# The gate and up products of a mixture of experts with weights stationary and 96 token slots moving, instead of 128 token slots stationary and weights moving

## The chip, the cores and the metric

The kernel runs on one core of a Trainium2 chip. The metric is the device time of one execution in microseconds (us). Lower is better.

## The reference, cut to what matters

The program is one inference step of a two-layer decoder on 280 tokens (16 meta tokens, 256 of a prompt, 8 samples). Each layer has a mixer and a feed-forward part. That of the second layer is a mixture of 8 experts, of which every token uses two:

```python
def swiglu(h, w1, w3, w2):
    return (jax.nn.silu(h @ w1) * (h @ w3)) @ w2

def moe_ffn(h, w_router, w1, w3, w2):
    logits = (h @ w_router).astype(jnp.float32)
    top_v, top_i = lax.top_k(logits, TOP_K)          # TOP_K = 2
    gates = jax.nn.softmax(top_v, axis=-1)
    combine = jnp.sum(jax.nn.one_hot(top_i, N_EXPERTS, dtype=jnp.float32) * gates[..., None], axis=-2)
    ...
    for e in range(N_EXPERTS):                        # 8 experts
        out = out + combine[..., e:e + 1] * swiglu(h, w1[e], w3[e], w2[e])
```

The model is 1024 wide (D), an expert 3584 (DE). All data are 32-bit floats. Counted on the reference's inputs, the eight experts get 67, 55, 68, 77, 73, 61, 77 and 82 tokens.

## The kernel before

**Precision.** For the experts a 32-bit value is split in a high part and a low part, `x = hi + lo`, both of the type fp32r, and a product is made of three matmuls: hi by hi, hi by lo, lo by hi (`split_products`). All matmuls go through the helper `mm` (line 526), so the profile gives them that line; transposes have lines of their own (1055 the gather, 1066 the selection, 1105 the activations). A matmul instruction has a stationary operand, which a weight load (PEld in the profile) brings in, and a moving one, whose columns stream through. Every matmul here has a weight load of its own.

**Stream of weights.** SyncE (SP) loads all weights through a ring of 7 slots of 128x2048 floats (1 MB). An expert has 3 x 14 slots, so the experts have 336. For each slot n ScalarE (ACT) writes the high part `w_hi[n % 4]` (`high`), VectorE (DVE) the low part `w_lo[n % 4]` (`low`) and gives the ring slot back (`weights_used`), and TensorE (PE) uses both. ACT may write `w_hi` for slot n + 4 when PE has finished slot n (`slot_done`).

**Iterations.** The 3584 columns of an expert are cut in 14 groups of FW = 256, so there are 8 x 14 = 112 iterations t. PE's program in one is written out by hand in `one_pass`: `up(t, 0)` and `up(t, 1)` with `turn(t - 1)` between them, then `down(t - 2)`.

- `up`: the gathered tokens of the expert (128 slots, CAP, most of the last ones empty) are stationary as `he_hi` and `he_lo`; the 256 gate and 256 up columns of the weights, side by side, are the 512 moving columns. Each of the two slots holds 4 of the 8 blocks of the contraction: 4 x 3 matmuls. The result is tokens by columns, in one PSUM bank.
- ACT makes silu of the gate half (`silu_out`), DVE multiplies by the up half (`act_out`), and PE turns the product with two transposes (`turn`), since the next product contracts over the columns. ACT and DVE split the turned result in `at_hi` and `at_lo` (`turned_out`).
- `down`: `at_hi` and `at_lo` stationary, 512 weight columns moving: 2 x 2 x 3 matmuls.

Once per expert, in fixed iterations of the 14: result times the token's weight (`y_out`), back to token order and added to x (`combine`, four iterations with 4 more matmuls each), which tokens the next expert gets (`rows_of`, with `select` on GpSimd), the fetch of their rows with an indirect DMA from GpSimd (POOL), and their transposes (`gather`). GpSimd does nothing else in this phase.

If an expert has more tokens than CAP, a second pass over all experts follows (`npass`).

Of the kernel before, what the change touches and what calls it, by code (L numbers as in the profile page):

```python
# [51 lines left out]
CAP = 128  # L52
# [71 lines left out]
def build(nc, a, debug=None):  # L124

    with ExitStack() as ctx:
# [52 lines left out]
        def ar(at, *shape):  # L179
# [4 lines left out]
            if len(shape) == 1:  # L184
# [62 lines left out]
        sil_e, act_e = ar(5504, 2, FW), ar(6016, 2, FW)  # L247
        y_hi, y_lo = half("y_hi", 4480, D), half("y_lo", 11840, D)
        he_hi = [half(f"he_hi{i}", 6720 + 2048 * i, DC, CAP) for i in range(2)]
        he_lo = [half(f"he_lo{i}", 7744 + 2048 * i, DC, CAP) for i in range(2)]  # L250
        at_hi, at_lo = half("at_hi", 10816, 2, 2 * CAP), half("at_lo", 11328, 2, 2 * CAP)

# [14 lines left out]
                 "selp_ready", "h_stored", "rows_ready", "he_in", "ey_hi", "ga_ps", "ga_hi", "ga_lo", "mw_ps", "mw_out", "eup_silu",  # L267
                 "eup_act", "et_ps", "et_hi", "et_lo", "ey_out", "em_ps", "em_out", "weights_used",
# [85 lines left out]
        def _(pool):  # L354
# [115 lines left out]
            def select(e):  # L470
                for m, (t0, nt, _) in enumerate(TILES):
                    ins = nc.gpsimd.tensor_scalar(sel_p[0:nt, m, :], iota[0:nt], place[0:nt, m, e + 1:e + 2],
                                                  chosen[0:nt, m, e + 1:e + 2], ALU.is_equal, ALU.mult)
                return ins
# [6 lines left out]

            def one_pass(p):
                for e in range(E):
                    n = p * E + e
                    if e or not isinstance(p, int):
                        pool.wait_ge(S["mw_ps"], n)
                        tick(p)
                    select(e).then_inc(S["selp_ready"], 1)
                    pool.wait_ge(S["mw_out"], n + 1)
                    tick(p)  # L490
                    if e or not isinstance(p, int):
                        pool.wait_ge(S["ga_ps"], p * (2 * E) + 2 * e)
                        tick(p)
                    else:
                        pool.wait_ge(S["h_stored"], 32)
                    nc.gpsimd.tensor_copy(rows[:], slot_iw[:, e % 2, 0:1]).then_inc(S["rows_ready"], 1)  # L496
                    pool.wait_ge(S["rows_ready"], n + 1)
                    tick(p)
                    nc.gpsimd.indirect_dma_start(he_f, None, h_rows, bass.IndirectOffsetOnAxis(ap=rows[:, 0:1], axis=0),
                                                 bounds_check=T - 1).then_inc(S["he_in"], 16)  # L500
# [23 lines left out]
        def _(pe):  # L524
# [523 lines left out]
            def gather(p, e, half_):  # L1048

                if half_ == 0:  # L1050
                    pe.wait_ge(S["he_in"], p * (16 * E) + 16 * (e + 1))
                    pe.wait_ge(S["em_out"], p * (E * DC) + DC * max(e - 1, 0))
                for j in range(4):
                    c = 4 * half_ + j
                    last = nc.tensor.transpose(pools[acc(e) + half_][:, j * P:(j + 1) * P], he_f[:, c * P:(c + 1) * P], ident[:])
                last.then_inc(S["ga_ps"], 1)

            def rows_of(p, e):

                pe.wait_ge(S["selp_ready"], p * E + (e + 1))  # L1060
                if e or not isinstance(p, int):
                    pe.wait_ge(S["mw_out"], p * E + e)
                for m, (t0, nt, _) in enumerate(TILES):
                    mm(pools[3][:, T:T + 2], sel_p[0:nt, m, :], id_w[0:nt, m, e, :], m == 0, m == 2)
                for m, (t0, nt, _) in enumerate(TILES):
                    last = nc.tensor.transpose(pools[3][:, t0:t0 + nt], sel_p[0:nt, m, :], ident[0:nt, 0:nt])
                last.then_inc(S["mw_ps"], 1)

            def combine(p, e, c0):
# [3 lines left out]
                for c in range(c0, c0 + 2):  # L1073
# [3 lines left out]
                    mm(o, y_hi[:, q], mix_s[e % 2], True, False)  # L1077
                    mm(o, y_lo[:, q], mix_s[e % 2], False, True).then_inc(S["em_ps"], 1)
# [6 lines left out]
            def up(p, t, part):  # L1085
# [4 lines left out]
                if part == 0 and t >= 2:  # L1090
                    pe.wait_ge(S["eup_act"], p * N_ITER + (t - 1))
# [1177 lines left out]
```

## Time and profile before

| | |
|---|---|
| median of 3 runs | 2256.25 us (2254.21 to 2258.53) |
| the profiled execution's own time | 2257.98 us |
| its span, first to last instruction | 2255.8 us |
| mean granted TensorE clock | 0.933 of full speed |
| busy: PE, PEld, DVE, ACT, POOL | 91%, 75%, 70%, 45%, 16% |
| moved from HBM | 459.74 MB |

The span is the time that the profile covers; the run's own time lies 2.2 us above it. A share of busy time is a mean over a mixer, a dense layer, a mixer and the experts, in which different engines matter; the experts take about the last 1020 us. A PE matmul's duration in the profile contains its latency, and the next one starts before it ends, so that the distance from start to start tells what a matmul costs in a stream.

### The profile page before, as it was taken

The page shows a single profiled execution, that of the slowest core. Times are in us where ns is not written, and L with a number is a line of the kernel's source. Part 1 is how long each engine was busy: PE and PEld are TensorE (multiplying, and loading weights), DVE is VectorE, ACT ScalarE, POOL GpSimd, SP SyncE. Part 2 cuts the span into 40 slices and gives each one's busy share as a digit, 9 for nine tenths or more (in the row PEclk, how much of TensorE's full clock was granted, in tenths as well). Part 3 has the DMA queues.
Part 4 walks back from the last instruction along what each step waited for, and adds up shares of the span by engine and source line. Part 5 has one row for each costly group of instructions (what it writes and reads, how often), then busy time and mean ns, then how long its engine had stood idle before and what let it go on. Part 6 is the DMA issues. An engine that isn't in the chain of part 4 may idle for free.

```text
span 2255.8 us, 29759 instructions
## 1 busy us (share of the span) xinstructions
PE 2056.7 (91%) x11490; PEld 1690.4 (75%) x11490; DVE 1573.3 (70%) x1960; ACT 1012.1 (45%) x1184; POOL 359.5 (16%) x315
## 2 busy tenths in 40 slices
PE   3998789898999997788895999999999999999996
PEld 2775577778999775577774888888888888888884
DVE  3586766325544777766324889898988889898984
ACT  1012323104433111333103777777767677777773
POOL 0553600200000554501201010101010100100000
PEclk7997999598999998999695999999999999999998
DMA  6333000144443333000142999999999999999990
GB/s 241 112 114 112 3 1 1 59 166 180 169 168 131 112 131 113 3 1 1 40 167 81 365 377 355 354 362 359 357 364 357 360 366 353 366 360 352 364 361 36
DMA packets 71627, 466.71 MB, mean 207 GB/s; under 512 B 12453, under 2 KB 13349, under 8 KB 16325
## 3 DMA queue, kind: packets, MB, share of 16 engines
q1 hardware_dynamic: 62352, 449.11, 53.7%
q0 software_dynamic: 3184, 13.24, 1.5%
q10 hardware_dynamic: 5956, 2.50, 0.4%
q8 instruction: 93, 1.52, 0.3%
q14 instruction: 42, 0.34, 0.0%
HBM read 459.74 MB, written 5.08 MB: 206 GB/s over the span
## 4 chain that ended last, share of the span: by engine, by line
PE 79%; DVE 7%; issue 6%; POOL 4%; ACT 2%; ACTq 1%; DMA 0%; SPq 0%; DVEq 0%; POOLq 0%
PE bank L526 77%; PE bank L1105 1%; ACTq L1183 1%; POOL arena L376 1%; DVE arena L1660 1%; PE bank L673 1%; ACT arena L1168 1%; POOL arena L390 1%; DVE arena L1490 0%; POOL arena L397 0%; DVE ring L1791 0%; DVE ring L1815 0%; DVE ring L1803 0%; ACT ring L1168 0%; POOL arena L408 0%
## 5 line engine op out<-in xcount | busy, mean ns | idle before, releaser
L2065 DVE TENSOR_TENSOR w_lo<-ring,w_hi 128x2048 fp32r<-128x2048 f32 x336 | 768.9, 2293 | 109.1 <-ACT w_hi L1168 108.7
L1168 ACT ACTIVATE w_hi<-ring 128x2048 fp32r<-128x2048 f32 x336 | 643.5, 1916 | 183.2 <-PE bank L526 183.2
L526 PE MATMUL bank<-arena,ring 128*128 128x280 f32 (+1 forms) x1920 | 460.6, 408 | 48.1 <-DVE arena L1490 23.0
L526 PEld LDWEIGHTS bank<-arena,ring 128*128 128x128 f32 (+1 forms) x1920 | 354.8, 190 | 143.4 <-issue 39.1
L1168 ACT ACTIVATE arena<-bank 128x256 f32<-128x256 f32 (+4 forms) x300 | 117.7, 396 | 592.2 <-PE bank L526 576.5
L526 PE MATMUL bank<-w_hi,he_hi 128*128 128x512 f32 x896 | 365.4, 408 | 4.9 <-DVE w_lo L2065 4.9
L526 PE MATMUL bank<-w_hi,he_lo 128*128 128x512 f32 x896 | 353.8, 395 | 0.0
L526 PE MATMUL bank<-w_lo,he_hi 128*128 128x512 f32 x896 | 353.4, 394 | 0.0
L526 PEld LDWEIGHTS bank<-w_hi,he_lo 128*128 128x128 f32 x896 | 169.0, 189 | 39.3
L526 PEld LDWEIGHTS bank<-w_hi,he_hi 128*128 128x128 f32 x896 | 169.1, 189 | 37.2 <-issue 5.3
L526 PEld LDWEIGHTS bank<-w_lo,he_hi 128*128 128x128 f32 x896 | 169.8, 190 | 32.4
L526 PE MATMUL bank<-ring 128*128 128x128 f32 (+6 forms) x1504 | 163.0, 269 | 31.9 <-DVE ring L1791 14.8
L526 PEld LDWEIGHTS bank<-ring 128*128 128x128 f32 (+3 forms) x1504 | 147.6, 171 | 49.7 <-DVE ring L1791 18.4
L526 PE MATMUL bank<-w_hi,at_hi 128*128 128x512 f32 x448 | 176.4, 394 | 0.0
L526 PE MATMUL bank<-w_hi,at_lo 128*128 128x512 f32 x448 | 176.4, 394 | 0.0
L526 PE MATMUL bank<-w_lo,at_hi 128*128 128x512 f32 x448 | 176.2, 393 | 0.0
L526 PE MATMUL bank<-arena 64*64 64x64 f32 (+12 forms) x1472 | 140.2, 307 | 34.8 <-DVE arena L1601 25.4
L526 PEld LDWEIGHTS bank<-arena 64*64 64x64 f32 (+6 forms) x1472 | 102.9, 179 | 76.5 <-issue 32.5
L1168 ACT ACTIVATE ring<-bank 128x256 f32<-128x256 f32 (+4 forms) x210 | 63.0, 358 | 169.2 <-PE bank L526 133.5
L496 POOL CAST rows<-arena 128x1 uint32<-128x1 f32 x8 | 13.9, 1732 | 763.9 <-ACT arena L1168 763.9
L1981 DVE TENSOR_TENSOR fw_lo<-ring,fw_hi 128x2048 fp32r<-128x2048 f32 x33 | 75.6, 2293 | 61.1 <-ACT fw_hi L1168 61.1
L526 PE MATMUL bank<-h_hi,fw_hi 128*128 128x280 f32 x352 | 103.6, 294 | 11.4 <-DVE fw_lo L1981 11.4
(261 smaller groups left out, 2634.9 us busy)
## 6 DMA issues: line engine op xcount, KB each, us to landing
ring<-wstream_dram SPq DMA_DIRECT2D x427, 1024.0 KB, 6.8
s<-s_dram POOLq DMA_DIRECT2D x2, 1024.0 KB, 14.7
o_rw_dram<-arena POOLq DMA_DIRECT2D x2, 1024.0 KB, 5.1
x<-x_dram SPq DMA_DIRECT2D x1, 1120.0 KB, 5.0
y_dram<-arena POOLq DMA_DIRECT2D x1, 1120.0 KB, 4.4
arena<-s_b_dram POOLq DMA_DIRECT2D x2, 512.0 KB, 7.5
arena<-s_c_dram POOLq DMA_DIRECT2D x2, 512.0 KB, 9.4
arena<-lora_up_dram POOLq DMA_DIRECT2D x2, 512.0 KB, 11.4
```

The lines of the kernel that those rows point to most:

```text
L376: g.tensor_tensor(tc, ca, cb, ALU.mult)
L390: ins = g.tensor_scalar(chi[:, f, :], z[:, 4 + f, :], col(l, "k_k", f), None, ALU.mult)
L496: nc.gpsimd.tensor_copy(rows[:], slot_iw[:, e % 2, 0:1]).then_inc(S["rows_ready"], 1)
L526: return nc.tensor.matmul(out, lhsT, rhs, start=start, stop=stop, **k)
L673: last = nc.tensor.transpose(pools[4 * i][0:nt, j * P:(j + 1) * P], src, ident[:])
L1105: last = nc.tensor.transpose(pools[2][:, (t % 2) * FW + j * P:(t % 2) * FW + (j + 1) * P], act_e[:, t % 2, j * P:(j + 1) * P], ident[:])
L1168: return nc.scalar.activation(out, in_, func, **k)
L1183: ac.dma_start(t[:], a[n]).then_inc(S["consts"], 16)
L1660: ins = v.tensor_scalar(z[:, c, :], z[:, c, :], col(l, "mu", c), None, ALU.mult)
L1981: v.tensor_tensor(fw_lo[n % 2], slot(FFN_AT + n), fw_hi[n % 2].bitcast(F32), ALU.subtract)\
L2065: v.tensor_tensor(w_lo[n % SPLIT], slot(n), w_hi[n % SPLIT].bitcast(F32), ALU.subtract)\
```

## The change

It leaves the rest of the program alone and does this in the expert phase:

- CAP goes from 128 to 96 slots. `he_hi` and `he_lo` become one tile `he` with the 96 high and the 96 low columns side by side for each of the 8 contraction blocks.
- `up` is turned around: a 128x128 block of gate or up weights is stationary. The high part of the block meets `he` whole (192 columns: hi and lo tokens), the low part meets the 96 high columns. `up(t, 0)` takes a slot with gate weights, `up(t, 1)` one with up weights, each 2 blocks of columns by 8 of the contraction. The result is columns by tokens in two banks, the products with the tokens' high part in one half and those with the low part in the other.
- `turn` and its transposes go. Instead the halves have to be added: ACT copies the low half of both banks to `sum_e` (`low_products`), DVE adds the other half (`sum_out`), ACT makes silu (`silu_out`), POOL multiplies (`act_out`), ACT writes `at_hi` (`act_high`), POOL `at_lo` (`act_low`).
- `down` has 96 stationary columns, otherwise as before; so have the other steps of an expert. `rows_of` uses the expert's own banks, and GpSimd's steps (`choose`, `fetch`) have fixed iterations.

```diff
-CAP = 128
+CAP = 96
...
+        he = [half(f"he{i}", 6720 + 1536 * i, DC, 2, CAP) for i in range(2)]
+        at_hi, at_lo = half("at_hi", 10816, 2, 2, CAP), half("at_lo", 11328, 2, 2, CAP)
+        def up_bank(t, u):
+            return pools[2 * (t % 2) + u][:, 0:4 * CAP].rearrange("p (b s t) -> p b s t", b=2, s=2)
+        def up_parts(t, s):
+            both = banks[:, 2 * (t % 2):2 * (t % 2) + 2, 0:4 * CAP]
+            return both.rearrange("p u (b s t) -> p u b s t", b=2, s=2)[:, :, :, s, :]
...
+            def act_out(p, t):
+                pool.wait_ge(S["eup_part"], up_part(p, t, "silu"))
+                nc.gpsimd.tensor_tensor(act_e[:, t % 2], sil_e[:, t % 2], sum_e[:, t % 2, 1], ALU.mult).then_inc(S["eup_act"], 1)
+            def act_low(p, t):
+                pool.wait_ge(S["et_hi"], p * N_ITER + (t + 1))
+                nc.gpsimd.tensor_tensor(at_lo[:, t % 2], act_e[:, t % 2], at_hi[:, t % 2].bitcast(F32), ALU.subtract)\
+                    .then_inc(S["et_lo"], 1)
...
                 if part == 0 and t >= 2:
-                    pe.wait_ge(S["eup_act"], p * N_ITER + (t - 1))
-                w_h, w_l = (w.rearrange("p (k m) -> p k m", k=DC // 2) for w in w_split(p, SLOT_OF[f"up{part}", t]))
-                for c in range(DC // 2):
-                    k = part * (DC // 2) + c
-                    last = split_products(pools[t % 2], (he_hi[e % 2][:, k, :], he_lo[e % 2][:, k, :]),
-                                          (w_h[:, c, :], w_l[:, c, :]), k == 0, k == DC - 1)
+                    pe.wait_ge(S["eup_sum"], p * N_ITER + (t - 1))
+                w_h, w_l = (w.rearrange("p (k m) -> p k m", k=DC) for w in w_split(p, SLOT_OF[f"up{part}", t]))
+                for b in range(2):
+                    o, q = up_bank(t, part)[:, b], slice(b * P, (b + 1) * P)
+                    for k in range(DC):
+                        if k < DC - 1:
+                            mm(o, w_h[:, k, q], he[e % 2][:, k], k == 0, False)
+                        last = mm(o[:, 1], w_l[:, k, q], he[e % 2][:, k, 0], False, False)
+                    last = mm(o, w_h[:, k, q], he[e % 2][:, k], False, True)
                 last.then_inc(S["slot_done"], 1)
-            def turn(p, t):
...
+            def low_products(p, t):
+                ac.wait_ge(S["slot_done"], p * N_SLOTS + (SLOT_OF["up1", t] + 1))
+                fn(sum_e[:, t % 2], up_parts(t, 1), ACT.Identity).then_inc(S["eup_part"], 1)
             def silu_out(p, t):
...
+                ac.wait_ge(S["eup_sum"], p * N_ITER + (t + 1))
+                fn(sil_e[:, t % 2], sum_e[:, t % 2, 0], ACT.Silu).then_inc(S["eup_part"], 1)
+            def act_high(p, t):
+                ac.wait_ge(S["eup_act"], p * N_ITER + (t + 1))
...
+            def sum_out(p, t):
+                dve.wait_ge(S["eup_part"], up_part(p, t, "low"))
+                v.tensor_tensor(sum_e[:, t % 2], sum_e[:, t % 2], up_parts(t, 0), ALU.add).then_inc(S["eup_sum"], 1)
```

**The order on PE.** In the expert phase of the kernel before, from `turn` into the second `up` of an iteration, PE's program reads as follows (the number behind a name is that of the buffer; the three matmuls come four times):

```order
L1105 MATMUL bank<-ident,arena 128x128 [waits et_lo,eup_act]
L1105 MATMUL bank<-ident,arena 128x128
L526 MATMUL bank<-w_hi_59,he_hi_69 128x512 [waits weights_used]
L526 MATMUL bank<-w_lo_63,he_hi_69 128x512
L526 MATMUL bank<-w_hi_59,he_lo_71 128x512
```

In the changed kernel the end of the second `up` of an iteration, `down`, and the start of the next `up` read:

```order
L563 MATMUL bank<-he_69,w_lo_66 128x96 x2
L563 MATMUL bank<-he_69,w_hi_62 128x192
L563 MATMUL bank<-w_hi_59,at_hi 96x512 [waits et_lo,weights_used]
L563 MATMUL bank<-w_lo_63,at_hi 96x512
L563 MATMUL bank<-w_hi_59,at_lo 96x512
L563 MATMUL bank<-he_69,w_hi_60 128x192 [waits weights_used,eup_sum]
L563 MATMUL bank<-he_69,w_lo_64 128x96
```

An `up` call had 12 matmuls of 512 moving columns and has 32, of 192 and 96 columns in turn; the transposes are gone, and `down` still has 12 of 512.

**The order on ACT.** In one iteration ACT had two small steps, one behind the other, among three splits of weights:

```order
L1168 ACTIVATE arena<-bank 128x256 [waits eup_act,slot_done]
L1168 ACTIVATE w_hi_62<-ring 128x2048 [waits slot_done,slot_in1]
L1168 ACTIVATE w_hi_59<-ring 128x2048 [waits slot_done,slot_in2]
L1168 ACTIVATE w_hi_60<-ring 128x2048 [waits slot_done,slot_in3]
L1168 ACTIVATE at_hi<-bank 128x256 [waits slot_done,et_ps]
```

In the changed kernel it has three, each between two splits:

```order
L1199 ACTIVATE arena<-bank 128x384 [waits slot_done]
L1199 ACTIVATE w_hi_62<-ring 128x2048 [waits slot_done,slot_in1]
L1199 ACTIVATE arena<-arena 128x192 [waits eup_sum]
L1199 ACTIVATE w_hi_59<-ring 128x2048 [waits slot_done,slot_in2]
L1199 ACTIVATE at_hi<-arena 128x192 [waits slot_done,eup_act]
L1199 ACTIVATE w_hi_60<-ring 128x2048 [waits slot_done,slot_in3]
```

The third small step now waits for POOL (`eup_act`), whose two new instructions per iteration are, in POOL's program:

```order
L520 TENSOR_TENSOR arena<-arena 128x192 [waits eup_part]
L524 TENSOR_TENSOR at_lo<-arena,at_hi 128x192 [waits et_hi]
L484 TENSOR_SCALAR arena<-iota,arena 128x96 [waits mw_ps]
L484 TENSOR_SCALAR arena<-iota,arena 128x96
L484 TENSOR_SCALAR arena<-iota,arena 24x96
```

The selection of the next expert's tokens (line 484) now stands behind the two small steps of an iteration; before it stood alone.

## Rows read from the trace of the kernel before

**Rows 1.** Busy time by stretch: columns us, PE, PEld, DVE, ACT, POOL, clock, DMA share, GB/s.

```profile
1300.00:2200.00 900.00, 900.00 (x4090) 732.98 (x4090) 801.93 (x593) 656.62 (x549) 57.64 (x32) 1.00 0.96 360
```

**Rows 2.** The chain that ended last, two iterations and a start; start, us, what.

```profile
1362.16 0.22 PE bank L1105 x2
1362.38 8.33 PE bank L526 x36
...
1370.93 8.34 PE bank L526 x36
...
1379.49 8.83 PE bank L526 x40
...
1503.67 8.84 PE bank L526 x40
```

**Rows 3.** Waits from 1300 to 2200 us: who, for whom, us, times, longest.

```profile
ACT w_hi L1168 <- PE bank L526: 168.5, 196, 1.9
DVE w_lo L2065 <- ACT w_hi L1168: 97.8, 277, 1.9
SPq L340 <- DVE w_lo L2065: 715.2, 304, 3.6
```

**Rows 4.** Timeline of PE and of its weight loads behind a turn.

```profile
1503.29 0.38 PE L1105 MATMUL bank<-ident,arena 128*128 128x128 f32 x2
1503.42 0.48 PE L526 MATMUL bank<-w_hi,he_hi 128*128 128x512 f32 x1
...
1503.40 0.19 PEld L526 LDWEIGHTS bank<-w_hi,he_hi 128*128 128x128 f32 x1
1503.51 0.19 PEld L526 LDWEIGHTS bank<-w_lo,he_hi 128*128 128x128 f32 x1
1503.74 0.19 PEld L526 LDWEIGHTS bank<-w_hi,he_lo 128*128 128x128 f32 x1
```

**Rows 5.** Busy time by stretch: the router's small matmuls, the dense layer, two mixer stretches.

```profile
1189.70:1197.30 7.60, 7.58 (x48) 7.56 (x48) 0.27 (x1) 0.00 (x0) 0.00 (x0) 0.50 0.00 0
530.00:700.00 170.00, 170.00 (x1322) 170.00 (x1321) 81.45 (x75) 66.55 (x70) 0.00 (x0) 1.00 0.49 174
290.00:330.00 40.00, 35.35 (x312) 28.68 (x312) 26.05 (x73) 12.53 (x40) 0.00 (x0) 1.00 0.00 1
1104.00:1118.00 14.00, 13.06 (x142) 12.81 (x142) 1.97 (x3) 0.59 (x1) 6.38 (x6) 0.50 0.01 1
```

**Rows 6.** Groups of PE and PEld instructions, whole run: busy, mean ns, idle.

```profile
L526 PE MATMUL bank<-router,arena 128*128 128x8 f32 x32 | 7.0, 362 | 6.1 <-DVE arena L1490 6.1
L526 PE MATMUL bank<-router,arena 128*24 128x8 f32 x16 | 0.8, 189 | 0.0
L526 PEld LDWEIGHTS bank<-w_hi,he_hi 128*128 128x128 f32 x896 | 169.1, 189 | 37.2 <-issue 5.3
L1105 PEld LDWEIGHTS bank<-ident,arena 128*128 128x128 f32 x224 | 31.4, 140 | 15.4
```

**Rows 7.** Timeline of the weight loads of plain 32-bit 128x128 matmuls in a mixer.

```profile
367.89 5.54 PEld L526 LDWEIGHTS bank<-ring 128*128 128x128 f32 x48 [1.26 <-DVE ring L1791]
```

**Rows 8.** Groups of DVE, ACT and POOL instructions, 1300 to 2200 us.

```profile
L2065 DVE TENSOR_TENSOR w_lo<-ring,w_hi 128x2048 fp32r<-128x2048 f32 x305 | 698.2, 2293 | 98.2 <-ACT w_hi L1168 97.8
L1168 ACT ACTIVATE w_hi<-ring 128x2048 fp32r<-128x2048 f32 x305 | 584.5, 1916 | 168.5 <-PE bank L526 168.5
L1168 ACT ACTIVATE arena<-bank 128x256 f32<-128x256 f32 x102 | 39.4, 386 | 75.4 <-PE bank L526 75.4
L1168 ACT ACTIVATE he_hi<-bank 128x512 fp32r<-128x512 f32 x14 | 8.1, 576 | 0.0
L2034 DVE TENSOR_TENSOR he_lo<-bank,he_hi 128x512 fp32r<-128x512 f32 x14 | 9.6, 683 | 0.0
L472 POOL TENSOR_SCALAR arena<-iota,arena 24x128 f32<-24x128 f32 x6 | 14.8, 2459 | 0.0
```

**Rows 9.** Timeline: DVE's splits of weights back to back.

```profile
1501.31 6.69 DVE L2065 TENSOR_TENSOR w_lo<-ring,w_hi 128x2048 fp32r<-128x2048 f32 x3
```

More of the change, by code:

```diff
@@ L480, in tick, with choose @@
                     nc.gpsimd.tensor_tensor(pool_tick[:, k:k + 1], iota[:, 0:1], iota[:, 1:2], ALU.add)
-            def one_pass(p):
[L483 to L500, printed above, removed]
+            def choose(p, e):
+                n = p * E + e
+                if e or not isinstance(p, int):
+                    pool.wait_ge(S["mw_ps"], n)
+                    tick(p)
+                select(e).then_inc(S["selp_ready"], 1)
@@ new lines, in fetch @@
+            def fetch(p, e):
+                n = p * E + e
+                pool.wait_ge(S["mw_out"], n + 1)
+                tick(p)
+                if e or not isinstance(p, int):
+                    pool.wait_ge(S["ga_ps"], p * (2 * E) + 2 * e)
+                    tick(p)
+                else:
+                    pool.wait_ge(S["h_stored"], 32)
+                nc.gpsimd.tensor_copy(rows[0:CAP], slot_iw[0:CAP, e % 2, 0:1]).then_inc(S["rows_ready"], 1)
+                pool.wait_ge(S["rows_ready"], n + 1)
+                tick(p)
+                nc.gpsimd.indirect_dma_start(he_f[0:CAP], None, h_rows, bass.IndirectOffsetOnAxis(ap=rows[0:CAP, 0:1], axis=0),
+                                             bounds_check=T - 1).then_inc(S["he_in"], 16)
@@ new lines, in act_out @@
+            def act_out(p, t):
[5 more added lines that the diff above has]
+                    .then_inc(S["et_lo"], 1)
+            def one_pass(p):
+                choose(p, 0)
+                fetch(p, 0)
+                for t in range(1, N_ITER + 1):
+                    e, g = divmod(t, NG)
+                    act_out(p, t - 1)
+                    act_low(p, t - 1)
+                    if e < E - 1 and g == G_YOUT:
+                        choose(p, e + 1)
+                    if e < E - 1 and g == G_ROWS + 1:
+                        fetch(p, e + 1)
@@ L1060, in rows_of @@
                 pe.wait_ge(S["selp_ready"], p * E + (e + 1))
+                if e >= 2:
+                    pe.wait_ge(S["em_out"], p * (E * DC) + DC * (e - 1))
+                if e == 0 and isinstance(p, int):
+                    pe.wait_ge(S["ht_out"], 6)
                 if e or not isinstance(p, int):
@@ L1432, in one_pass @@
                     if 1 <= t <= N_ITER:
[L1433 removed]
+                        silu_out(p, t - 1)
                     if t < N_ITER:
[L1435 removed]
                         high_after(p, SLOT_OF["up1", t])
+                    if 1 <= t <= N_ITER:
+                        act_high(p, t - 1)
                     if t >= LAG:
@@ L2196, in _stream @@
     assert slots.shape[0] == S_DENSE
-    up = np.stack([i[w][0].reshape(E, DC, P, NG, FW).transpose(0, 3, 2, 1, 4) for w in ("moe_w1", "moe_w3")], 4)
-    up = up.reshape(N_ITER, P, 2, SLOT)
+    up = [i[w][0].reshape(E, DC, P, NG, FW).transpose(0, 3, 2, 1, 4).reshape(N_ITER, P, SLOT) for w in ("moe_w1", "moe_w3")]
     down = i["moe_w2"][0].reshape(E, NG, 2, P, D).transpose(0, 1, 3, 2, 4).reshape(N_ITER, P, SLOT)
     experts = np.empty((N_SLOTS, P, SLOT), np.float32)
-    parts = {"up0": up[:, :, 0], "up1": up[:, :, 1], "down": down}
+    parts = {"up0": up[0], "up1": up[1], "down": down}
     for n, (kind, t) in enumerate(ORDER):
```

83 lines of the change are left out of this document (28 added, 55 removed).

## The prediction

> **What bounds the kernel now.** I read the busy time by stretch first. From 1300 to 2200 us, all of it expert phase, PE is busy in 900 of 900 us at the full clock, DVE in 802, ACT in 657, POOL in 58, and the DMA share is 0.96 [rows 1]. Three engines are near their limit there, so the share alone doesn't say which one sets the pace. The waits do: ACT waits for PE 168.5 us, DVE for ACT 97.8 us, SP for DVE 715.2 us, and PE has no row of waits in this stretch [rows 3]. The chain of work is PE alone: 36 matmuls in 8.34 us, two transposes in 0.22 us, and so on [rows 2]. The reader is to see that every other engine waits, directly or through another, for PE.
>
> So the price list of PE decides. A matmul of 512 columns costs 8.34 / 36 = 0.2317 us, and an iteration 8.34 + 0.22 = 8.56 us. Four iterations of an expert have 4 matmuls more (the pieces of 40 [rows 2]); from the start of one such run of four to the next are 14 iterations and 1503.67 - 1379.49 = 124.18 us, 8.87 us each, and 112 of them make 993 us. In the dense layer a matmul of 280 columns costs 170 / 1322 = 0.1286 us [rows 5]. The line between both is 0.00044 us per column, by which 192 columns would cost 0.0895 us and 96 columns 0.047 us, if nothing else took longer.
>
> **What else takes longer: the weight load.** Each matmul has a load of 128 columns. With 512 moving columns it is hidden, which is why the trace of before shows its cost in few places only. Behind the two transposes of a turn, the load for the first matmul starts at 1503.40 and the next load at 1503.51, 0.11 us on; the third follows only at 1503.74, when the long matmul lets it [rows 4]. The router shows the same for a stream: 32 matmuls with 128 stationary columns and 16 with 24, all with 8 moving columns [rows 6], take 7.60 us at a clock of 0.50 [rows 5]. Eight moving columns cost next to nothing, so this is the price of the loads: 32 x 128 + 16 x 24 = 4480 columns in 7.60 us are 0.217 us per 128 columns, 0.1086 us at the full clock. Both rows give 0.109 us, and I take it. The plain 32-bit matmuls of 128x128 load 48 times in 5.54 us, 0.115 us each [rows 7]; their own streaming takes as long as the load, so this is the upper bound for a pair.
>
> A load starts when the matmul before has started (that is what the stream with 0.23 us distance shows [rows 4]), so that a pair of load and matmul costs the longer of the two: 0.109 us, for 192 columns (0.0895) as for 96 (0.047). The columns saved by the change are columns in which PE would wait for the load.
>
> The Trainium skill has this as a rule (TensorE: Matmul & The Clock Gate, section LDWEIGHTS): a load takes its number of columns divided by 1.2 GHz, whatever the rows, 107 ns for 128 columns. By it `up` would be 64 x 0.107 = 6.85 us. The trace agrees, with 0.109 us.
>
> **The change part by part, per iteration.**
> - Removed: 24 matmuls of 512 columns, 24 x 0.2317 = 5.56 us, and the turn, 0.22 us. Together 5.78 us.
> - Added: 2 slots x 2 blocks x 8 x 2 = 64 pairs of load and matmul, 64 x 0.109 = 6.98 us.
> - `down`: still 12 matmuls of 512 columns, 2.78 us; 96 instead of 128 stationary columns shorten a load that was hidden already.
> - Sum: 6.98 + 2.78 = 9.76 us instead of 8.56, +1.20 us. Times 112: +134 us.
> - Once per expert: the transposes of the gather and the selection have 96 slots for 128, in 8 and 6 short matmuls; a quarter of some 0.1 us each would be 0.3 us per expert, and since loads of 128 columns stay among them I take 1 us off in all. `combine` keeps its 280 columns. The start (selection, fetch, gather) and the end keep their chains.
>
> Hidden, and by what: ACT's work becomes 3 x 1.916 for the splits, about 0.48 for the copy of 384 columns (between 0.386 for 256 and 0.576 for 512), and two steps of at most 0.39 us, 7.0 us of 9.76. DVE's is 3 x 2.293 plus under 0.68 us for the sum, 7.5 us [rows 8]. The DMA has to bring 3.15 MB in 9.76 us, 322 GB/s, where it brings 360 now [rows 1]. All three get slacker. The new chain (copy, sum, silu, product, high part, low part) has to be done before `down(t)`, which starts a whole iteration and both `up` calls behind `up(t, 1)`, 9.76 + 6.98 = 16.7 us; its own steps, with 2.5 us for each of POOL's (its longest mean in this phase [rows 8]), are 0.48 + 0.68 + 0.39 + 2.5 + 0.39 + 2.5 = 6.9 us, and with three splits of 1.92 us that stand in between on ACT 12.7 us. The new wait of PE (`eup_sum`, two iterations back) is met long before. Without that cover, each us by which the chain were late would cost 112 us in all. At the end of the phase nothing new is late: two `down` calls, 5.56 us, stand between the last `up` and the last `down`, against 6.9 us, of which POOL's part shrinks when DVE's splits have ended. I book nothing there.
>
> No second pass: the fullest expert has 82 tokens, under 96.
>
> Against the profiled execution's 2257.98 us: + 134 - 1 gives 2391 us. It was 1.7 us above the median, so the forecast for a median is 2389 us.
>
> **The bounds.** The two digits of [rows 4] allow some 5 ns less than 0.11 us. With 0.105 us per pair the iteration is 9.50 us, +105 us: 2362. With 0.115 us it is 10.15 us, +178 us: 2433. Stalls that no row prices (a semaphore wait at a slot's start, a late split) could add some 15 us above: 2360 to 2450.
>
> **The rivals.**
> - *The loads are cheap, and the kernel gets faster.* The load of a transpose shows 140 ns where that of an fp32r matmul shows 189 [rows 6], 49 ns less. Did the new loads cost only 0.109 - 0.049 = 0.060 us, `up` would be 32 x (0.0895 + 0.060) = 4.78 us and PE's iteration 7.56 us. Then the DMA would bind: 360 GB/s at a share of 0.96 is 375 GB/s at most, 3.15 MB in 8.39 us. 112 x (8.87 - 8.39) = 54 us less: 2204 us. It turns from loss to gain where a pair costs (8.56 - 2.78) / 64 = 0.090 us. Against it stands that the loads of 0.11 us in [rows 4] are of just this type. A second rule of the Trainium skill points to this side (same page, section Back-to-back issue gap): a stream of load and matmul with 128 columns runs at about 81 ns a pair. By it `up` would be 64 x 0.081 = 5.18 us, an estimate, PE's iteration 7.96 us, and the end again at the DMA. The trace doesn't agree: the router's loads give 0.109 us.
> - *The clock falls.* While PE waits for loads, fewer columns stream. The granted clock was 0.50 from 1104 to 1118 us although PE shows 13.06 us busy of 14, and 1.00 from 290 to 330 us with 312 small matmuls [rows 5]; so a busy PE is no guarantee. At 0.50 an iteration would be 64 x 0.217 + 12 x 0.463 = 19.4 us, +1,220 us: about 3480 us. For the full clock speaks that there are no gaps, and that 12 long matmuls come in every iteration.
> - *POOL is shut out by DVE.* POOL's selection of 24x128 takes 2.46 us in this phase [rows 8], beside DVE's splits. The Trainium skill says why (GPSIMD Engine Reference, Key points): both share SBUF interfaces, which DVE instructions with two SBUF inputs contend for; the row agrees. ACT waits for POOL's product before `act_high`, behind which the next split stands. One split of 1.92 us hides the product, and ACT has 9.76 - 7.0 = 2.8 us to spare, so it decides from 4.7 us per POOL instruction. Were it shut out for three splits of DVE on end, 6.69 us [rows 9], ACT would need 7.0 + 6.69 - 1.92 = 11.8 us, +2.0 us: about 2616 us. Since DVE would be idle in 2.3 of 9.76 us, I doubt it.
>
> **How the numbers follow.** Load-bound at the full clock 0.83; cheap loads 0.07 (a tenth of it near the turning point); a fallen clock 0.05; POOL 0.05. The prediction is the first case, 2389 us, and its own bounds, 2360 to 2450, are the range; the other cases are what is left out. A measurement of this kernel can tell about 0.2%, 4.5 us, from no change. Faster 0.06, same 0.01, slower 0.93.
>
> **What would show it.** In the changed kernel's profile: PE still without waits in the expert phase; weight loads 0.109 us from start to start within `up`, for both widths; 7.0 us per two `up` calls, 2.8 us per `down`; about 1127 us for the 112 iterations with their extras (993 + 134); PEld busy near 100%; ACT and DVE idle longer for PE; DMA near 320 GB/s; clock 1.00. The prediction is wrong if the loads stand closer than 0.10 us, if the clock shows 0.50 in the phase, or if PE waits for `et_lo`, `eup_sum` or a split.

## The result and the profile after

| | before | after |
|---|---|---|
| median | 2257.33 us (2254.21 to 2258.53) | 2419.39 us (2417.52 to 2420.49) |
| span of the profiled execution | 2255.8 us | 2417.1 us |
| mean granted TensorE clock | 0.933 | 0.931 |
| the router's last matmul to the first `up` matmul | 34.5 us | 33.1 us |
| first `up` matmul to first `down` matmul | 19.7 us | 41.0 us |
| first `down` matmul to last | 971.7 us | 1115.6 us |
| plain iteration, from `down` to `down` (median) | 8.56 us | 9.89 us |

The ratio is 1.072, with a 95% interval from 1.070 to 1.074: the change makes the kernel slower by 7%. The lower four rows are distances between PE's starts in the two traces. A plain iteration is one in which PE does nothing for an expert's once-only steps (no combining, selection or gather). The whole difference of the spans, 161.3 us, is made of four parts: the first `up` matmul comes 4.0 us earlier, the stretch to the first `down` is 21.3 us longer, the stretch from there to the last `down` 143.9 us longer, and 32.7 us follow behind it in both. Of the 4.0 us only 1.3 lie between the router and the first `up`. The other 2.7 lie in the part before, where both kernels run the same program: there the router's last matmul starts anywhere from 1194.3 to 1199.6 us in the 13 traces of this document.

The busy time by stretch of the changed kernel (us, then PE, PEld, DVE, ACT and POOL, granted clock, DMA share, GB/s) has one stretch at the start and one of the steady part; the second answers to [rows 1]:

```profile
1237.00:1272.00 35.00, 35.00 (x158) 33.94 (x158) 13.26 (x8) 12.71 (x12) 6.65 (x4) 0.50 0.52 183
...
1300.00:2350.00 1050.00, 1050.00 (x8079) 963.94 (x8078) 794.34 (x498) 700.69 (x663) 550.22 (x240) 1.00 0.86 313
```

From 1300 us on PE is busy without a gap at the full clock. DVE, ACT and the DMA have become slacker: DVE is busy in 76% instead of 89%, ACT in 67% instead of 73%, and the DMA moves 313 GB/s instead of 360. GpSimd, which got new work, is busy in 52% instead of 6%. From 1237 to 1272 us PE is busy throughout too, but the granted clock is 0.50. In the kernel before it was 1.00 in just that stretch:

```profile
1237.00:1272.00 35.00, 35.00 (x156) 28.47 (x155) 30.26 (x22) 27.13 (x23) 0.00 (x0) 1.00 0.99 364
```

The waits of the changed kernel from 1300 to 2350 us (who, for whom, us, times, longest) answer to [rows 3]:

```profile
POOL arena L520 <- ACT arena L1199: 383.9, 98, 5.1
ACT w_hi L1199 <- PE bank L563: 349.7, 304, 2.1
DVE w_lo L2095 <- ACT w_hi L1199: 256.5, 304, 2.0
```

Before its splits ACT waits for PE in 33% of the stretch instead of 19%, DVE for ACT in 24% instead of 11%, and PE has no row. Its weight loads in the middle of an `up`, in the timeline:

```profile
1499.89 0.19 PEld L563 LDWEIGHTS bank<-he,w_hi 128*128 128x128 f32 x1
1500.00 0.19 PEld L563 LDWEIGHTS bank<-he,w_lo 128*128 128x128 f32 x1
1500.11 0.19 PEld L563 LDWEIGHTS bank<-he,w_hi 128*128 128x128 f32 x1
1500.22 0.19 PEld L563 LDWEIGHTS bank<-he,w_lo 128*128 128x128 f32 x1
```

The loads start 0.11 us apart whether the matmul between them streams 192 columns or 96. Over all of them the most frequent distances are 0.111 and 0.112 us. The columns of the start values matter here, not the 0.19 us behind them, which contain the load's latency. At the start of the phase the same pairs stand twice as far apart, as the matmuls show:

```profile
1235.36 0.49 PE L563 MATMUL bank<-he,w_hi 128*128 128x192 f32 x1
1235.65 0.34 PE L563 MATMUL bank<-he,w_lo 128*128 128x96 f32 x1
1235.79 0.49 PE L563 MATMUL bank<-he,w_hi 128*128 128x192 f32 x1
```

Two pairs in 0.43 us here, two in 0.22 us later.

### The profile page after: what moved, and what is told of

The parts are those of the page before. It is cut to its first block, busy times and chain, and to the rows that moved or that the text cites. A ratio compares the mean times of both kernels' runs of the same rounds, so it can differ in the third digit from the quotient of the medians.

```text
span 2417.1 us, 38165 instructions
## 1 busy us (share of the span) xinstructions
PE 2218.0 (92%) x15746; PEld 1944.6 (80%) x15746; DVE 1550.3 (64%) x1848; ACT 1047.8 (43%) x1296; POOL 885.5 (37%) x539
## 4 chain that ended last, share of the span: by engine, by line
PE 84%; DVE 7%; POOL 4%; issue 2%; ACT 2%; ACTq 1%; DMA 0%; SPq 0%; DVEq 0%; POOLq 0%
PE bank L563 82%; ACTq L1214 1%; POOL arena L388 1%; DVE arena L1527 1%; ACT arena L1199 1%; DVE arena L1697 1%; PE bank L710 0%; POOL arena L402 0%; POOL arena L409 0%; DVE ring L1828 0%; DVE ring L1852 0%; DVE ring L1840 0%; DVE rstd L1525 0%; ACT ring L1199 0%; POOL arena L420 0%
## 5 line engine op out<-in xcount | busy, mean ns | idle before, releaser
L563 PE MATMUL bank<-he,w_hi 128*128 128x192 f32 x3584 | 828.8, 318 | 4.8 <-DVE w_lo L2095 4.8
L563 PE MATMUL bank<-he,w_lo 128*128 128x96 f32 x3584 | 763.6, 239 | 0.0
L563 PEld LDWEIGHTS bank<-he,w_hi 128*128 128x128 f32 x3584 | 673.5, 196 | 9.4 <-issue 5.1
L563 PEld LDWEIGHTS bank<-he,w_lo 128*128 128x128 f32 x3584 | 664.9, 196 | 2.7
L520 POOL TENSOR_TENSOR arena<-arena 128x192 f32<-128x192 f32 x112 | 267.9, 2392 | 441.9 <-ACT arena L1199 441.9
L1199 ACT ACTIVATE arena<-bank 128x280 f32<-128x280 f32 (+5 forms) x300 | 126.7, 429 | 507.7 <-PE bank L563 491.9
L524 POOL TENSOR_TENSOR at_lo<-arena,at_hi 128x192 fp32r<-128x192 f32 x112 | 271.2, 2421 | 128.3 <-ACT at_hi L1199 128.3
L563 PE MATMUL bank<-w_hi,at_hi 128*96 128x512 f32 x448 | 176.5, 394 | 0.0
L563 PE MATMUL bank<-w_hi,at_lo 128*96 128x512 f32 x448 | 176.5, 394 | 0.0
L563 PE MATMUL bank<-w_lo,at_hi 128*96 128x512 f32 x448 | 176.0, 393 | 0.0
```

The costliest lines, as they stand in the source:

```text
L520: nc.gpsimd.tensor_tensor(act_e[:, t % 2], sil_e[:, t % 2], sum_e[:, t % 2, 1], ALU.mult).then_inc(S["eup_act"], 1)
L524: nc.gpsimd.tensor_tensor(at_lo[:, t % 2], act_e[:, t % 2], at_hi[:, t % 2].bitcast(F32), ALU.subtract)\
L563: return nc.tensor.matmul(out, lhsT, rhs, start=start, stop=stop, **k)
L1199: return nc.scalar.activation(out, in_, func, **k)
```

## The experiments

"Before" and "after" are the two kernels. Each median is of timed runs, and each ratio is against the kernel before on the same chip. Distances between starts of loads are those that are usual in the expert phase of the trace; a plain iteration is a median, and a mean iteration is taken over the 84 iterations of the second to the seventh expert.

**1. Fewer columns (e1_hi_96).** Is it the load that paces `up`, or the columns? For six of the eight contraction blocks the high part meets only the 96 high columns; the product of the weights' high part with the tokens' low part is left out there.

```diff
-                        if k < DC - 1:
-                            mm(o, w_h[:, k, q], he[e % 2][:, k], k == 0, False)
+                        if k == 0:
+                            mm(o, w_h[:, k, q], he[e % 2][:, k], True, False)
+                        elif k < DC - 1:
+                            mm(o[:, 0], w_h[:, k, q], he[e % 2][:, k, 0], False, False)
```

> It leaves out, in 6 of the 8 contraction blocks of up, the product of the weights' high part with the tokens' low part: those matmuls stream 96 columns instead of 192, and the number of weight loads stays 64 per iteration. Theory loads (a pair of load and matmul costs the load, 0.112 us in the changed kernel's trace): the same time as the changed kernel, 2419 us, within 5 us. Theory columns (the streamed columns set the pace): 24 x 96 columns less per iteration at 0.00044 us each are 1.02 us, 114 us in all, so about 2305 us.

Measured: 2431.92 us, ratio 1.077 (1.074 to 1.081). The plain iteration is 9.90 us, as in after, so these columns are free at the full clock, and the theory of the columns falls. But fewer columns made the whole slower, by 12.5 us. The busy time by stretch shows where:

```profile
1590.00:1611.00 21.00, 21.00 (x163) 19.13 (x162) 16.31 (x13) 13.59 (x14) 9.82 (x4) 1.00 0.83 297
1611.00:1624.70 13.70, 13.70 (x56) 12.21 (x56) 5.90 (x4) 4.33 (x4) 4.25 (x2) 0.50 0.58 228
...
2188.00:2201.70 13.70, 13.70 (x54) 12.03 (x55) 5.72 (x4) 4.33 (x4) 4.82 (x2) 0.51 0.57 220
```

Twice, in the midst of an uninterrupted stream of PE, the clock falls to its lower level of 1.2 GHz for 13.7 us. Each time half of the stretch is lost, 2 x 6.85 = 13.7 us in all, about what the run was longer. Of the four executions the one with a mean clock of 0.930, which is that of after, took 2422.18 us; the three at 0.923 to 0.925 took 2431 to 2436 us.

**2. More columns (e2_cap128).** The same question from the other side: 128 slots, so 256 and 128 moving columns.

```diff
-CAP = 96
+CAP = 128
-        sum_e = ar(9792, 2, 2, 2, CAP)
+        sum_e = ar(13888, 2, 2, 2, CAP)
-        he = [half(f"he{i}", 6720 + 1536 * i, DC, 2, CAP) for i in range(2)]
+        he = [half(f"he{i}", 6720 + 2048 * i, DC, 2, CAP) for i in range(2)]
```

> The changed kernel with 128 token slots instead of 96: 256 and 128 moving columns. Theory loads: the 128-column matmuls still cost the load, 0.112 us, the 256-column ones 0.118 us by the line through 0.1286 (280 columns) and 0.2317 us (512), so 32 x 0.006 = 0.2 us more per iteration, 22 us in all: about 2441 us. Theory columns: a third more columns in up, 32 x 96 columns x 0.00044 us = 1.35 us per iteration, 151 us more: about 2570 us.

Measured: 2430.96 us, ratio 1.078 (1.076 to 1.080). A third more columns cost 11.6 us in all. The loads' distances are now 0.109 us in front of a low part and 0.121 in front of a high one, 0.115 on average, and the plain iteration is 10.13 us. The first `down` to the last takes 26.5 us more than in after, near the 22 that the theory of the loads gave. That the total grew by less comes from the start: the first `up` to the first `down` takes 24.7 us instead of 41.0, because the clock rises there. Busy time by stretch of this kernel:

```profile
1228.00:1234.00 6.00, 5.18 (x25) 5.21 (x25) 6.00 (x4) 3.75 (x3) 0.00 (x0) 0.50 0.68 244
1234.00:1253.00 19.00, 19.00 (x166) 19.00 (x165) 12.60 (x8) 12.86 (x11) 4.24 (x3) 0.99 0.88 323
```

So the load binds at 192 and 96 columns, and at 256 the columns begin to show.

**3. Small steps on DVE (e3_on_dve).** The product and the low part (`act_out`, `act_low`) go from GpSimd to DVE, behind the same waits; the cut leaves out their place in DVE's order.

```diff
-                nc.gpsimd.tensor_tensor(act_e[:, t % 2], sil_e[:, t % 2], sum_e[:, t % 2, 1], ALU.mult).then_inc(S["eup_act"], 1)
+                v.tensor_tensor(act_e[:, t % 2], sil_e[:, t % 2], sum_e[:, t % 2, 1], ALU.mult).then_inc(S["eup_act"], 1)
...
-                nc.gpsimd.tensor_tensor(at_lo[:, t % 2], act_e[:, t % 2], at_hi[:, t % 2].bitcast(F32), ALU.subtract)\
+                v.tensor_tensor(at_lo[:, t % 2], act_e[:, t % 2], at_hi[:, t % 2].bitcast(F32), ALU.subtract)\
```

> The changed kernel with the two small steps (product, low part) on VectorE instead of GpSimd. Theory loads: they are hidden, VectorE has some 2.4 us to spare per iteration and gets about 0.7 us of work: 2419 us, within 5 us. Rival (GpSimd's 2.4 us per instruction and its traffic cost the weight loads or the chain something): faster, by up to the 24 us by which the result lies above my load price, so down to 2395 us, with loads 0.109 us apart.

Measured: 2421.14 us, ratio 1.073 (1.071 to 1.075), the plain iteration 9.89 us. GpSimd neither costs nor gives anything while PE is the bound.

**4. Grouped order (e4_grouped).** All eight high parts of a block of columns first, then the eight low parts.

```diff
-                        if k < DC - 1:
-                            mm(o, w_h[:, k, q], he[e % 2][:, k], k == 0, False)
-                        last = mm(o[:, 1], w_l[:, k, q], he[e % 2][:, k, 0], False, False)
-                    last = mm(o, w_h[:, k, q], he[e % 2][:, k], False, True)
+                        mm(o, w_h[:, k, q], he[e % 2][:, k], k == 0, False)
+                    for k in range(DC):
+                        last = mm(o[:, 1], w_l[:, k, q], he[e % 2][:, k, 0], False, k == DC - 1)
```

> The changed kernel with the order of the matmuls changed: for each block of 128 columns first the 8 high parts of the weights (192 moving columns each), then the 8 low parts (96 each). Theory loads: each pair costs its load in either order, 2419 us, within 5 us. Rival (the alternation of long and short matmuls costs the 3 ns between the 0.109 us that I took and the 0.112 us in the trace): about 2397 us, with loads 0.109 us apart.

Measured: 2420.56 us, ratio 1.073 (1.071 to 1.075). The loads still start 0.112 us apart: the change between widths or operands costs nothing, and isn't what makes a pair 0.111 instead of 0.109 us.

**5. Half the pairs (e5_no_low).** `up` leaves out the 32 pairs with the weights' low part. What binds next?

```diff
-                        if k < DC - 1:
-                            mm(o, w_h[:, k, q], he[e % 2][:, k], k == 0, False)
-                        last = mm(o[:, 1], w_l[:, k, q], he[e % 2][:, k, 0], False, False)
-                    last = mm(o, w_h[:, k, q], he[e % 2][:, k], False, True)
+                        last = mm(o, w_h[:, k, q], he[e % 2][:, k], k == 0, k == DC - 1)
```

> It leaves out the products of the weights' low part in gate and up (the low part is still written): 32 pairs per iteration instead of 64. Theory loads: PE's plain iteration falls from 9.89 us by 32 x 0.111 = 3.56 us to 6.3 us, 6.6 with an expert's other work, and something else sets the pace: the transfers, 3.15 MB per iteration at 375 GB/s or 8.39 us by the row of before (360 GB/s at a share of 0.96), about 2204 us. So it shows where a cheaper up would end at best. Rival (PE still bound, for example by another price per pair): between 2204 and 2420 us with PE busy throughout.

Measured: 2236.73 us, ratio 0.990 (0.989 to 0.992). That is 183 us less than after: with half of the pairs gone, so is the whole loss. But it isn't the 2204 us that I expected, so the transfers alone don't set the pace. Waits from 1300 to 2150 us:

```profile
PEld bank L563 <- DVE w_lo L2092: 145.0, 116, 7.0
PE bank L563 <- POOL at_lo L524: 133.5, 83, 6.9
```

PE now waits for DVE's splits, and in `down` for GpSimd; its clock is 0.96 in the mean and the mean iteration 8.69 us. So this total doesn't give the price of a pair; it shows that fewer pairs take the loss away.

**6. A cheaper load (e7_low_bf16_grouped).** The low parts of gate and up weights are written as bf16 and meet a bf16 copy of the tokens, which ACT writes in the gather; grouped as in 4. The columns stay as they are, the type changes.

```diff
+        w_lo_b = [nc.alloc_sbuf_tensor_at(f"w_lo_b{i}", [P, SLOT], BF16, offset=arena_at + 4 * at).ap()
...
-                return w_hi[n % SPLIT], w_lo[n % SPLIT]
+                return w_hi[n % SPLIT], (w_lo if ORDER[n][0] == "down" else w_lo_b)[n % SPLIT]
...
+                        mm(o, w_h[:, k, q], he[e % 2][:, k], k == 0, False)
+                    for k in range(DC):
+                        last = mm(o[:, 1], w_l[:, k, q], he_b[e % 2][:, k], False, k == DC - 1)
```

> The changed kernel with the low part of the gate and up weights in bfloat16, against a bfloat16 copy of the tokens; the 8 low parts stand behind the 8 high parts. It tells whether the price of a load hangs on the type. Theory loads with a price by type: a bfloat16 load of 128 columns costs no more than the 0.06 us that a transpose's load shows, so up is 32 x 0.111 + 32 x 0.06 = 5.5 us, PE's iteration 8.25 us and with the other work 8.53 us: just above the transfers' 8.39 us, about 2215 us. Rival (the price is 128 columns whatever the type): 2419 us.

Measured: 2227.54 us, ratio 0.987 (0.985 to 0.989). The loads in the timeline, eight of each kind together:

```profile
1400.41 0.37 PEld L568 LDWEIGHTS bank<-he_b,w_lo_b 128*128 128x128 bf16 x8
1400.72 0.97 PEld L568 LDWEIGHTS bank<-he,w_hi 128*128 128x128 f32 x8
1401.70 0.37 PEld L568 LDWEIGHTS bank<-he_b,w_lo_b 128*128 128x128 bf16 x8
```

A bf16 pair costs 0.043 us, an fp32r pair 0.111 still; from the last fp32r load to the first bf16 one are 0.200 us. The 0.043 us are about what the prediction's line gives for 96 columns (0.047), so they are an upper bound for the bf16 load alone. The plain iteration falls to 7.93 us, but the total lies 12 us above the 2215 that I expected: the mean iteration is 8.63 us. Part of the difference is the other work of an expert (8.21 us in experiment 11), the rest is a wait that comes once per expert. The chain there, start, us and what:

```profile
1368.28 0.37 ACT at_hi L1203
...
1368.72 7.91 POOL at_lo L529
1376.64 0.14 issue
1376.77 3.32 PE bank L568 x8
```

GpSimd's small subtraction, 2.1 to 2.5 us as a rule, takes 7.9 us seven times from 1300 us on, once per expert, and PE waits 4.98 us for it. In that time DVE's timeline has two-input instructions back to back:

```profile
1367.71 1.40 DVE L2089 SCALAR_TENSOR_TENSOR y_lo<-bank,arena,y_hi 96x512 fp32r<-96x512 f32 x2
1369.03 2.28 DVE L2101 TENSOR_TENSOR w_lo<-ring,w_hi 128x2048 fp32r<-128x2048 f32 x1
1371.23 2.28 DVE L2101 TENSOR_TENSOR w_lo_b<-ring,w_hi 128x2048 bf16<-128x2048 f32 x1
1373.43 0.55 DVE L2083 TENSOR_TENSOR arena<-arena,bank 128x384 f32<-128x384 f32 x1
1373.89 2.28 DVE L2101 TENSOR_TENSOR w_lo_b<-ring,w_hi 128x2048 bf16<-128x2048 f32 x1
```

After shows what a GpSimd step of this size costs without DVE. The first of these two stands in a gap of DVE, which ends an instruction at 1563.96 us and starts the next at 1565.25; the second runs beside one:

```profile
1564.33 0.59 POOL L520 TENSOR_TENSOR arena<-arena 128x192 f32<-128x192 f32 x1
1565.54 2.46 POOL L524 TENSOR_TENSOR at_lo<-arena,at_hi 128x192 fp32r<-128x192 f32 x1 [0.62 <-ACT at_hi L1199]
```

In the expert phase of kernel 6 the subtraction takes 0.59 to 0.60 us in the 10 cases in which DVE is idle all the while. The 2.5 us with which the prediction reckoned were a time beside DVE too: the selection they were read from takes 0.8 us in before where DVE is idle (1215 to 1222 us). The profile's times of GpSimd are rough, but the three levels, 0.6, 2.1 to 2.5 and 7.9 us, lie far apart.

**7. The same in turn (e6_low_bf16).** As 6, but in the order of the change, a high part and a low part in turn.

```diff
-                        last = mm(o[:, 1], w_l[:, k, q], he[e % 2][:, k, 0], False, False)
+                        last = mm(o[:, 1], w_l[:, k, q], he_b[e % 2][:, k], False, False)
```

> The low part of the gate and up weights in bfloat16, in the order of the changed kernel: high (192 columns) and low (96 columns) in turn. Grouped, a low pair took 0.043 us and a high one 0.111 us. Theory overlap (a load runs beside the matmul before it, whatever the types): each two pairs cost 0.0895 us (the high matmul, over the low load) + 0.111 us (the high load), 32 x 0.20 = 6.4 us per iteration, about 2325 us. Theory switch (a bfloat16 load starts only when the fp32r matmul before it has streamed; the grouped kernel's trace has 0.200 us from the last high load to the first low one, 0.111 + 0.0895): at least 0.200 + 0.043 us for two pairs, 7.8 us per iteration, about 2480 us, slower than with fp32r low parts.

Measured: 2361.55 us, ratio 1.047 (1.045 to 1.048), the plain iteration 9.39 us: neither number. The loads in the timeline:

```profile
1502.39 0.10 PEld L568 LDWEIGHTS bank<-he_b,w_lo_b 128*128 128x128 bf16 x1
1502.40 0.20 PEld L568 LDWEIGHTS bank<-he,w_hi 128*128 128x128 f32 x1
1502.61 0.10 PEld L568 LDWEIGHTS bank<-he_b,w_lo_b 128*128 128x128 bf16 x1
```

Both start within 0.01 us, the next two 0.21 us later (0.2155 in the mean), where a bf16 and an fp32r pair in their own groups cost 0.043 + 0.111 = 0.154. A change of type and back costs some 0.06 us together, so the order matters as soon as the types differ. What causes it stays open.

**8. 96 slots alone (e8_before_96).** The kernel before with only its slots cut to 96. The lines left out here cut the shapes of the tiles to it.

```diff
-CAP = 128
+CAP = 96
...
```

> The kernel before with 96 token slots instead of 128, tokens stationary and weights moving as they were; one part of the change alone. PE still streams 36 x 512 columns per iteration and the shorter loads were hidden: the time of before, 2256 us, within 5 us. Rival (the slots matter for PE): a quarter off the streaming is not possible since they are not the moving side, so only a cheaper turn and gather, at most 0.1 us per iteration, 11 us less.

Measured: 2246.76 us, ratio 0.996 (0.994 to 0.997). That is 11 us less, outside the 5 us that I allowed and at the size of the rival, which put it to a cheaper turn and gather. In the traces the first `down` to the last takes 8.1 us less, and the plain iteration 8.51 us instead of 8.56. From the router's last matmul to the first `up` this kernel takes 33.2 us, after 33.1; with 128 slots it is 34.5 in before and 34.5 in experiment 2 too. So the slots are worth 1.3 us at the start, and the rest of the 4.0 us by which `up` began earlier is no effect of the change.

This kernel also shows that the price of a load goes with its columns. Behind a turn, where before had 0.11 us from load to load with 128 columns, two loads of 96 columns start 0.08 us apart (0.082 most often in the whole trace):

```profile
1504.96 0.16 PEld L526 LDWEIGHTS bank<-w_hi,he_hi 128*96 128x96 f32 x1
1505.04 0.17 PEld L526 LDWEIGHTS bank<-w_lo,he_hi 128*96 128x96 f32 x1
```

By columns that is 0.109 us for 128, so what binds isn't a fixed price of a pair of instructions.

**9. The clock at the start (e9_warm).** After, with 14 plain 32-bit matmuls of 512 columns on constants, 8 and 6 of them around the gather's transposes; their result isn't used. The trace shows them as 28 instructions, 0.43 us apart at the full clock.

```diff
                 rows_of(p, 0)
+                warm(8)
                 gather(p, 0, 0)
                 gather(p, 0, 1)
+                warm(6)
```

> The changed kernel with 14 extra matmuls of 512 plain 32-bit columns (constants, into a bank that is not yet used) while PE waits for the first expert's rows and splits. In the changed kernel the granted clock stays at 0.50 from 1204 to 1272 us, 45 us into the stream of up; in that of before it rises at 1237 us. Theory clock: the start of the phase at half clock costs 16 to 18 us; with the clock up at the first matmul of up the time is about 2402 us. Rival (the new stream pulls the clock down by itself): the clock falls again before the first down, and the time stays at 2419 us or more.

Measured: 2403.11 us, ratio 1.064 (1.062 to 1.066), 16.3 us less than after. Two stretches of this kernel:

```profile
1204.00:1237.00 33.00, 23.26 (x92) 14.64 (x93) 10.80 (x28) 10.44 (x11) 3.33 (x5) 0.74 0.19 68
1237.00:1272.00 35.00, 35.00 (x291) 33.40 (x290) 26.97 (x15) 23.81 (x22) 17.65 (x9) 1.00 0.93 347
```

In the second one PE does 291 matmuls where after did 158. The first `up` to the first `down` takes 21.6 us instead of 41.0, and the first iteration behind it 9.88 instead of 11.47; `up` itself starts 6.0 us later. 19.4 + 1.6 - 6.0 = 15.0 us, and the spans differ by 14.9. Of the 6.0 us only 1.5 lie behind the router's last matmul, where the extra matmuls stand; 4.5 lie before it, in the scatter named above. So with the clock up the expert phase gets 19.5 us shorter, and the clock makes the start long.

**10 and 11. GpSimd in the way (e13_bf16_low_dve, e12_bf16_both_dve).** Kernel 6 with the low part on DVE (10), and with both small steps there (11); the edits are those of 3.

> The grouped bfloat16 kernel with only the last small step (the low part of the activations) on VectorE, the product still on GpSimd. Theory GpSimd: VectorE has 8.2 us of work, the transfers need 8.39 us, PE 8.2 us; the product can be shut out once per expert, but PE's down no longer waits for GpSimd directly: 8.45 us per iteration, about 2208 us. Rival (the product is shut out as the low part was, and ACT waits for it): 2220 us or more, with ACT waiting over 4 us at a time for GpSimd.

> The grouped bfloat16 kernel (2227.5 us) with both small steps on VectorE. There, once per expert, GpSimd's low part took 7.9 us while VectorE ran one instruction behind the other, PE waited 5 us, and the clock fell for 3 to 7 us. Theory GpSimd: these waits of PE go, but VectorE has now 3 x 2.29 + 0.54 + 2 x 0.35 + 0.40 = 8.5 us of work per iteration and sets the pace: 8.52 against 8.63 us, 12 us less, about 2216 us. Rival (VectorE as the bound has waits of its own): 2227 us or more.

Measured: 2199.77 us, ratio 0.975 (0.973 to 0.976), with the low part moved, and 2182.53 us, ratio 0.967 (0.965 to 0.968), with both. The mean iteration falls from 8.63 to 8.37 and 8.21 us, the plain one stays at 7.93 us. Both are below what I expected (2208 and 2216 us), and the order of the two came out the other way round. Busy time by stretch of the last kernel:

```profile
1300.00:2150.00 850.00, 846.93 (x8050) 755.16 (x8047) 828.26 (x707) 706.72 (x675) 82.91 (x28) 1.00 0.96 378
```

PE is busy in all but 3 of 850 us and the clock is 1.00. This version beats both kernels, by 3.3% and 9.8% (its low products of gate and up are those of bf16 operands). My expectation for it was too high because it added DVE's durations: they overlap. In this stretch they add up to 876 us, and DVE is busy in only 828. The DMA moves 378 GB/s, more than the 375 that the prediction took as its end.

## Why the prediction held, step by step

- **PE's price list decides, and the load binds.** Right. After shows PE without waits and 0.11 us between loads of either width; experiments 1 and 4 change columns and order without effect on the plain iteration, 5 takes half of the pairs away and gets 183 us back, and 6 and 8 show that the price goes with the type and the columns of the stationary operand. That speaks against the rule of the Trainium skill which I gave as the rival (TensorE: Matmul & The Clock Gate, Back-to-back issue gap, 81 ns a pair): this kernel shows 111. The rule of the Trainium skill for the load (same page, section LDWEIGHTS, 107 ns for 128 columns) comes within 4% of it at the full clock. At a granted clock of 0.50 the pairs of this kernel took twice as long, 0.215 us, which that rule doesn't give.
- **0.109 us per pair.** Right in kind, short by 2%. The plain iteration is 9.89 us where 9.76 was forecast, 0.13 us / 64 = 2 ns a pair. It grew by 1.34 us, and so did the combining ones (from 9.08 to 10.41 us); some of the others grew a little less. Behind the first `down` stand 109 full iterations. The first of them, part of it at the lower clock, grew by 2.9 us, the other 108 by 1.31 us in the mean, 141.3 us; with 0.3 us less between the last two `down` calls that is the 143.9 us measured. The forecast had 109 x 1.20 = 131 us for this. Why the stream runs at 0.111 to 0.112, where a load behind a turn and some in experiment 2 take 0.109, is open: the order (4) and GpSimd (3) are ruled out. The upper bound of 0.115 rested on plain 32-bit matmuls streaming as long as they load; 9 bears that out, with 0.43 us for 512 columns, a quarter of which is 0.107.
- **The start keeps its chain.** This is the term that was missing. The chain was the same, but the first three iterations' `up` ran at 1.2 GHz: 21.3 us were added where the forecast had 3 x 1.20 = 3.6. The rival of the fallen clock named the mechanism and put it at the whole phase or nowhere. The kernel before already had 0.50 at its first matmuls, and the clock rose at 1237 us, between 5 and 6 us into its 512-column matmuls; after streams 192 and 96 columns from 1227.7 us on and gets the full clock only at 1272. Experiment 9 shows that it is the clock. What in the stream makes it late wasn't varied by itself, and the traces only allow a comparison. The clock rose within 5 to 7 us of the first `up` matmul with 256 and 128 columns (2), with pairs of 192 columns alone (5) and with grouped bf16 low parts (6). It took 44 to 46 us with fp32r pairs of 192 and 96 columns, in turn (after, 3) or grouped (4), and 39 us with bf16 in turn (7). With 96 columns in most pairs (1) it took 46 us and was lost twice in mid-stream. That the short columns keep it down fits all of these but is inferred from them.
- **1 us off for the gather.** At the start it was 1.3 us, and comes with 96 slots in the kernel before as well (8). The other 2.7 us by which `up` began earlier are scatter of the part before, so they are luck in the comparison of the two traces.
- **GpSimd and the new chain hidden.** Right here: 2.42 and 2.45 us per instruction, 2.47 at most from 1300 us on, no wait of PE, no change without it (3). The rival's mechanism shows in 6, with 7.9 us beside DVE's two-input instructions, and 10 and 11 get 28 and 45 us back by moving the steps away. The Trainium skill says that GpSimd and VectorE share SBUF interfaces, for which DVE instructions with two SBUF inputs contend (GPSIMD Engine Reference, Key points), and the trace agrees: 0.59 us without DVE, 2.1 and more beside it. In after, where DVE is idle in 24% of the time, no such long step occurred; whether the kernel could have absorbed one was not tested.
- **The end.** 32.7 us after the last `down` in both, as booked.
- **Signs.** No wait of PE, DMA at 313 for 320 GB/s, clock 1.00 from 1300 us: right. But a clock of 0.50 in the phase was on the list of what would show the prediction wrong, and it was there for the first 44 us. 1156.7 us from the first `up` to the last `down` for the 1127 forecast. PEld is busy in 92%, not near 100%: it idles between the long matmuls of `down`.

The sum is 133 us forecast against 161 us between the two traces (162 between the medians): 13 more from the iterations and 18 more from the start, less 3 from the earlier first `up`, nearly all of it scatter. The iterations' part lies inside the range that the prediction gave for the price of a pair. The start's 18 us were no term of the range, which only left room for 15 us of stalls; that 2419 us falls well inside it is in that part luck. One small slip of the sum: by its own steps 0.105 us per pair gives 2361 us for a median, not 2362, which changes nothing.

## What to carry to other kernels

When the weights become the stationary operand, count the loads, not the columns: a load costs the same for few moving columns as for many, and below the width where streaming takes as long (here some 240 columns, by 0.111 us and 0.00044 us a column) it sets the price. Check the type of that operand first, since a pair with a bf16 one took 0.043 us here, well under half, and keep types in groups. Before a start that came earlier or later in a trace is put down to a change, measure it from the last point that both kernels share. At the head of a phase look at the granted clock, and ask whether the new matmuls bring it up as the old ones did.

## What the hardware showed that I had not expected

- PE busy in 35 of 35 us and a granted clock of 0.50, for 44 us on end, with fp32r pairs of 192 and 96 columns; with 96 columns in most of them, two falls to 0.50 in mid-stream (1).
- Pairs of 0.043 us with bf16 weights and 96 columns, against 0.111 with fp32r. The Trainium skill has a faster load for types other than fp32 (TensorE: Matmul & The Clock Gate, Weight-path perf modes), and the trace agrees as to which type is the faster; whether that mode was at work here no run shows.
- bf16 and fp32r in turn cost 0.2155 us for two pairs instead of 0.154 (7).
- A GpSimd step of 128x192 takes 0.59 us while DVE is idle, 2.1 to 2.5 us beside a DVE instruction, and in 6 it took 7.9 us when DVE ran one two-input instruction behind the other.
- The part of the program before the router, the same in all kernels, ended up to 5.3 us apart in the 13 traces.
